# A transformer-style layer kernel on one core: x loaded first, conditioning row chunks shared out differently, late columns placed amid lower steps

## The reference, cut to what matters

```python
c_act = jax.nn.silu(c)
mod = (c_act @ w_ada[l] + b_ada[l])[:, None, :]
sh_m, sc_m, g_m, sh_f, sc_f, g_f = jnp.split(mod, 6, axis=-1)
u = layer_norm(x) * (1 + sc_m) + sh_m
z = u @ w_in[l]
```

## Time and profile before

| | us |
|---|---|
| median of 3 runs | 1427.4 (1426.52 to 1428.69) |
| the profiled execution, its own time | 1426.88 |
| its span in the trace | 1425.1 |
| TensorE busy in the span | 1393.0 (98%) |
| VectorE / ScalarE / GpSimd busy | 969.4 / 647.3 / 421.8 |

### The profile page before, as it was taken

One profiled execution on the slowest core, in us unless ns is written; L12 is line 12 of the kernel. 1 busy time (PEld: TensorE's weight loads), 2 busy tenths in 40 slices (PEclk: granted clock), 3 DMA queues, 4 the chain that ended last, 5 costly groups with the idle time before them and its releaser, 6 DMA issues.

```text
span 1425.1 us, 17299 instructions
## 1 busy us (share of the span) xinstructions
PE 1393.0 (98%) x6522; PEld 1148.6 (81%) x6522; DVE 969.4 (68%) x1340; ACT 647.3 (45%) x914; POOL 421.8 (30%) x453
## 2 busy tenths in 40 slices
PE   7799999999999999999999999999999999999996
PEld 3688888888888888888888888888888888888885
DVE  5789677776479946464768797556565646437787
ACT  5522677777542124101616774443345535343251
POOL 1006465555566000000024327333444200001315
PEclk9899999999999999999999999999999999999998
DMA  9775465654565232762622555444445878456361
GB/s 347 266 266 159 148 185 156 188 168 149 161 234 172 89 104 79 245 192 86 200 114 89 183 181 193 142 145 146 156 163 207 297 277 299 162 211 236 118 222 60
DMA packets 159083, 256.42 MB, mean 180 GB/s; under 512 B 11352, under 2 KB 81422, under 8 KB 159000
## 3 DMA queue, kind: packets, MB, share of 16 engines
q1 hardware_dynamic: 144152, 204.97, 43.1%
q0 software_dynamic: 14848, 50.34, 10.5%
HBM read 182.36 MB, written 68.71 MB: 176 GB/s over the span
## 4 chain that ended last, share of the span: by engine, by line
PE 91%; DVE 5%; ACT 2%; issue 1%; DMA 1%; SPq 0%; DVEq 0%; ACTq 0%
PE ps L2065 24%; PE ps L2067 24%; PE ps L2066 24%; PE ps L2214 11%; PE ps L2254 2%; PE ps L2264 2%; PE ps L2279 2%; PE ps L2085 1%; DVE part_lo L1922 1%; PE ps L2129 1%; PE ps L2404 1%; DVE q L1983 0%; DMA k_raw<-tw_scratch 0%; DMA ada<-in_w_ada_dram 0%; DVE w_lo L1387 0%
## 5 line engine op out<-in xcount | busy, mean ns | idle before, releaser
L2065 PE MATMUL ps<-act_hi,w_hi 128*128 128x512 f32 (+1 forms) x480 | 187.2, 390 | 9.4 <-DVE act_lo L1482 9.4
L1922 DVE TENSOR_TENSOR part_lo<-k_raw,part_hi 128x1024 fp32r<-128x1024 f32 x112 | 146.1, 1332 | 58.6 <-ACT part_hi L935 55.4
L2067 PE MATMUL ps<-act_hi,w_lo 128*128 128x512 f32 (+1 forms) x480 | 184.6, 385 | 0.0
L2066 PE MATMUL ps<-act_lo,w_hi 128*128 128x512 f32 (+1 forms) x480 | 184.6, 385 | 0.0
L2065 PE MATMUL ps<-part_hi 128*128 128x512 f32 x448 | 174.3, 389 | 0.0
L2066 PE MATMUL ps<-part_lo,part_hi 128*128 128x512 f32 x448 | 174.3, 389 | 0.0
L2067 PE MATMUL ps<-part_hi,part_lo 128*128 128x512 f32 x448 | 174.3, 389 | 0.0
L935 ACT ACTIVATE part_hi<-k_raw 128x1024 fp32r<-128x1024 f32 x112 | 116.4, 1059 | 113.6 <-DMA k_raw<-tw_scratch 48.8
L2065 PEld LDWEIGHTS ps<-act_hi,w_hi 128*128 128x128 f32 x480 | 91.1, 190 | 28.4 <-issue 5.9
L1387 DVE TENSOR_TENSOR w_lo<-w_raw,w_hi 128x1024 fp32r<-128x1024 f32 x51 | 65.9, 1291 | 65.6 <-ACT w_hi L935 65.6
L2066 PEld LDWEIGHTS ps<-act_lo,w_hi 128*128 128x128 f32 x480 | 91.2, 190 | 18.4 <-issue 1.0
(11 more groups left out here) (260 smaller groups left out, 3202.4 us busy)
## 6 DMA issues: line engine op xcount, KB each, us to landing
k_raw<-h_scratch SPq DMA_DIRECT2D x112, 256.0 KB, 4.2
w_raw<-in_w_in_dram SPq DMA_DIRECT2D x42, 512.0 KB, 4.1
ada<-in_w_ada_dram SPq DMA_DIRECT2D x8, 2048.0 KB, 9.6
tw_rows<-in_w_ff_dram POOLq DMA_DIRECT2D x64, 256.0 KB, 4.1
tw_scratch<-tw_sum POOLq DMA_DIRECT2D x32, 512.0 KB, 3.7
h_scratch<-h_sum POOLq DMA_DIRECT2D x64, 256.0 KB, 3.0
k_raw<-tw_scratch SPq DMA_DIRECT2D x64, 256.0 KB, 5.4
pair_raw<-in_w_ff_dram SPq DMA_DIRECT2D x13, 1024.0 KB, 6.3
```

Source lines behind the costliest of these rows:

```text
L1922: nc.vector.tensor_tensor(part_lo[s][:, :, :], k_raw[rs][:, :, :], f(part_hi[s][:, :, :]), ALU.subtract)\
L2065: nc.tensor.matmul(out, sh, mh, start=first, stop=False)
L2066: nc.tensor.matmul(out, sh, ml, start=False, stop=False)
L2067: return nc.tensor.matmul(out, sl, mh, start=False, stop=last)
```

## The change

- SP loads all of x ahead of chunk 0. Weight block 1 goes ahead of chunk 1, and block 2, which waits for VectorE's first `cut_lo`, ahead of chunk 3.
- TensorE turns tiles 0 to 4 first, then chunk 0's first half, tiles 5 and 6, its second half, tile 7, the small rows, six of chunk 2's eight rows, and the columns of 0 and 2. Behind them stand 24 transposes of the identity into a bank that nothing reads, in three groups of 8; the second group waits for `mod_done` 1, the third for the first `modulate_x`.
- The last two rows of chunk 2 are summed on VectorE; `row_columns(2)` adds both parts, 8 small matmuls in place of 4.
- Chunk 3 is split: rows 0 to 3 on TensorE behind the lower steps of blocks 0 and 1, rows 4 to 7 on VectorE. `row_columns(3)` has 8 small matmuls in place of 4. The columns of 1 and 3 stand after two of block 2's four lower steps.
- ScalarE and VectorE go tile by tile instead of by pairs; tiles 6 and 7 are both copied by VectorE.

The diff, cut to its core:

```diff
-N_DIRECT = 2
+N_DIRECT = 1
+SPLIT = {0: 4, 1: 4, 2: 6, 3: 4}
...
-ADA_BANKS = {0: 0, 2: 1}
+ADA_BANKS = {0: 0, 2: 1, 3: 6}
...
                 elif i == 4:
-                    sp.wait_ge(partial_done, 1)
+                    sp.wait_ge(partial_done, 2)
                 elif i == 5:
                     sp.wait_ge(head_ps_done, 4)
+                    sp.wait_ge(partial_done, 1)
                 elif i == 6:
-                    sp.wait_ge(partial_done, 2)
+                    sp.wait_ge(head_ps_done, 5)
+                    sp.wait_ge(partial_done, 3)
...
-                ks = slice(4 * half, 4 * half + 4)
+                ks = (slice(0, SPLIT[i]), slice(SPLIT[i], 8))[half]
...
-            load_ada_half(0, 0)
-            load_x(range(2))
-            load_ada_half(0, 1)
-            load_x(range(2, 4))
+            load_x(range(ST))
+            load_ada(0)
...
-            load_ada_half(2, 0)
-            load_x(range(4, 6))
-            load_ada_half(2, 1)
-            load_x(range(6, ST))
+            load_ada(2)
             load_block(0)
+            load_block(1)
             load_ada(1)
-            load_block(1)
+            load_block(2)
             load_ada(3)
-            load_block(2)
...
-            for i in range(0, ST, 2):
+            for i in range(ST):
                 take_root(i, i)
-                take_root(i + 1, i + 1)
-                norm(i, i, mid[:, i, :])
-                if i + 1 < ST - 1:
-                    norm(i + 1, i + 1, mid[:, i + 1, :])
-                if i == 2:
-                    save_ada_row(0)
-                if i == ST - 2:
-                    save_ada_row(2)
-                    cut_hi(0)
-                    save_tile(i)
-                else:
-                    save_tile(i)
-                    save_tile(i + 1)
+                if i >= 1:
+                    norm(i - 1, i - 1, mid[:, i - 1, :])
+                if i >= 2:
+                    save_tile(i - 2)
+            save_ada_row(0)
+            save_ada_row(2)
+            cut_hi(0)
...
             cut_hi(2)
+            save_ada_row(3)
             act.wait_ge(mod_done, 2)
...
-            for i in range(0, ST, 2):
-                for t in (i, i + 1):
-                    dve.wait_ge(x_in[t], 16)
-                    stats(mid[:, t, :], t)
-                for t in (i, i + 1):
-                    scale_bias(t, t)
-                if i == 4:
-                    dve.wait_ge(head_ps_done, 3)
-                    nc.vector.tensor_copy(cols[:, 0:ROWS_A], ps[:, 7, PIECE:PIECE + ROWS_A])
-                    nc.vector.tensor_copy(cols[:, ROWS_A:ROWS_A + ROWS_C], ps[:, 7, PIECE + P:PIECE + P + ROWS_C])\
-                        .then_inc(cols_done, 1)
+            for t in range(ST):
+                dve.wait_ge(x_in[t], 16)
+                stats(mid[:, t, :], t)
+                if t >= 1:
+                    scale_bias(t - 1, t - 1)
+            scale_bias(ST - 1, ST - 1)
...
-                dve.wait_ge(ada_in[i % 3], 16 * (i // 3 + 1))
+                if i == 1:
+                    dve.wait_ge(ada_in[1], 16)
+                elif i in (2, 3):
+                    dve.wait_ge(ada_end_in[i % 3], 16 * (i // 3 + 1))
+                else:
+                    dve.wait_ge(ada_in[i % 3], 16 * (i // 3 + 1))
...
             def end_chunk(i):
-                if i in (1, 3):
-                    dve.wait_ge(ada_end_in[i % 3], 16 * (i // 3 + 1))
-                add_rows(i, range(4, 8))
+                if i == 1:
+                    dve.wait_ge(ada_end_in[1], 16)
+                add_rows(i, range({2: 7, 3: 5}.get(i, 4), 8))
...
+            for t in (ST - 2, ST - 1):
+                dve.wait_ge(z_done, t + 1)
+                dve.wait_ge(x_copied, ST - 2)
+                nc.vector.tensor_copy(x_t[:, :, t * P:(t + 1) * P], tile_banks(t)).then_inc(x_copied, 1)
+            dve.wait_ge(head_ps_done, 3)
+            nc.vector.tensor_copy(cols[:, 0:ROWS_A], ps[:, 7, PIECE:PIECE + ROWS_A])
+            nc.vector.tensor_copy(cols[:, ROWS_A:ROWS_A + ROWS_C], ps[:, 7, PIECE + P:PIECE + P + ROWS_C])\
+                .then_inc(cols_done, 1)
+            ada_chunk(2)
             mixer_columns(0)
-            dve.wait_ge(z_done, ST)
-            nc.vector.tensor_copy(x_t[:, :, (ST - 1) * P:ST * P], tile_banks(ST - 1)).then_inc(x_copied, 1)
             cut_lo(0)
...
-                pe.wait_ge((ada_in, ada_end_in)[half][i % 3], 16)
-                for k in range(4 * half, 4 * half + 4):
+                pe.wait_ge((ada_in, ada_end_in)[half][i % 3], 32 if i == 3 else 16)
+                for k in range(4 if half else 0, 8 if half else SPLIT[i]):
                     ins = nc.tensor.matmul(ps[0:1, ADA_BANKS[i], :], c_act[:, k:k + 1], ada[i % 3][:, k, :],
-                                           start=k == 0, stop=k == 7)
+                                           start=k == 0, stop=k == (7, None, 5, 3)[i])
                 return ins
...
             def row_columns(i):
 
-                if i in (0, 2):
-                    pe.wait_ge(head_sb_done, 3 + i // 2)
-                else:
+                if i != 1:
+                    pe.wait_ge(head_sb_done, {0: 3, 2: 4, 3: 5}[i])
+                if i > 0:
+                    pe.wait_ge(partial_done, {2: 1, 1: 2, 3: 3}[i])
+                if i in (1, 3):
                     pe.wait_ge(cols_done, 1)
-                    pe.wait_ge(partial_done, 1 + i // 2)
                 for m in range(4):
                     out, ms = ps[:, 6 + i % 2, 4 * i + m:4 * i + m + 1], slice(m * P, (m + 1) * P)
-                    if i in (0, 2):
-                        ins = nc.tensor.matmul(out, ada_row[i][:, ms], ones_row[0:1, 0:1], start=True, stop=True)
-                    else:
-                        ins = nc.tensor.matmul(out, partial_of(i)[:, ms], ones_row[:, 0:1], start=True, stop=True)
+                    if i != 1:
+                        ins = nc.tensor.matmul(out, ada_row[i][:, ms], ones_row[0:1, 0:1], start=True, stop=i == 0)
+                    if i > 0:
+                        ins = nc.tensor.matmul(out, partial_of(i)[:, ms], ones_row[:, 0:1], start=i == 1, stop=True)
                 ins.then_inc(reduced, 1)
...
+            for i in range(5):
+                transpose_x(i)
             pe.wait_ge(head_sb_done, 2)
             row_chunk(0, 0)
-            transpose_x(0)
-            transpose_x(1)
+            transpose_x(5)
+            transpose_x(6)
             row_chunk(0, 1).then_inc(head_ps_done, 1)
-            transpose_x(2)
-            transpose_x(3)
+            transpose_x(7)
             pe.wait_ge(small_in, SMALL_ROWS)
...
-            row_chunk(2, 0)
-            transpose_x(4)
+            row_chunk(2, 0).then_inc(head_ps_done, 1)
             row_columns(0)
-            transpose_x(5)
-            row_chunk(2, 1).then_inc(head_ps_done, 1)
-            transpose_x(6)
             row_columns(2)
-            transpose_x(7)
+
+            def keep_active():
+                for m in range(8):
+                    nc.tensor.transpose(ps[:, 0, m % 4 * P:(m % 4 + 1) * P], ident[:, :], ident[:, :])
+
+            keep_active()
+            pe.wait_ge(mod_done, 1)
+            keep_active()
+            pe.wait_ge(u_step, 1)
+            keep_active()
 
             def rows_part(n, k):
                 pe.wait_ge(u_lo_done, k + 1)
@@ -2167,11 +2176,15 @@
             for n in range(2):
                 for k in range(2, 4):
                     rows_part(n, k)
+            pe.wait_ge(mod_done, 1)
+            row_chunk(3, 0).then_inc(head_ps_done, 1)
             pe.wait_ge(w_lo_done, 3)
-            for k in range(4):
+            for k in range(2):
                 rows_part(2, k)
             row_columns(1)
             row_columns(3)
+            for k in range(2, 4):
```

More of the change, by code:

```diff
@@ L962, in save_ada_row @@
             def save_ada_row(i):
-                act.wait_ge(head_ps_done, {0: 1, 2: 4}[i])
+                act.wait_ge(head_ps_done, {0: 1, 2: 4, 3: 5}[i])
                 copy(ada_row[i], ps[0:1, ADA_BANKS[i], :]).then_inc(head_sb_done, 1)
@@ L1434, in start_chunk @@
                     dve.wait_ge(reduced, i - 3)
-                link(nc.vector.tensor_scalar(partial_of(i)[:, :], ada[i % 3][:, 0, :], c_act[:, 0:1], None, ALU.mult))
-                add_rows(i, range(1, 4))
+                k0 = SPLIT[i] if i in (2, 3) else 0
+                link(nc.vector.tensor_scalar(partial_of(i)[:, :], ada[i % 3][:, k0, :], c_act[:, k0:k0 + 1], None,
+                                             ALU.mult))
+                add_rows(i, range(k0 + 1, 4))
             def end_chunk(i):
-                if i in (1, 3):
-                    dve.wait_ge(ada_end_in[i % 3], 16 * (i // 3 + 1))
-                add_rows(i, range(4, 8))
+                if i == 1:
+                    dve.wait_ge(ada_end_in[1], 16)
+                add_rows(i, range({2: 7, 3: 5}.get(i, 4), 8))
             def add_rows(i, ks):
@@ L2174, in _ @@
             row_columns(3)
```

(2 more changed lines are left out.)

## The result

The changed kernel takes 1431.97 us (median of 8 runs, 1430.70 to 1433.91) against 1427.34 (8 runs, 1426.52 to 1428.69) for the kernel before: ratio 1.0032, 95% interval 1.0022 to 1.0042. It is slower by 4.6 us (3.1 to 6.0). The forecast was 1431.6, slower. The traced execution of the changed kernel took 1432.93 us with a span of 1431.1, 6.0 more than the span before; so its trace shows the loss a little large.

A forecast was written before the change was run, and what follows sets the result against it. TensorE, busy almost throughout, was taken as the bound, so delays in the early stages reach the end almost whole. Head 3.8 plus late columns 0.4 gave 4.2 us, hence 1431.6 us; own range 1430.0 to 1433.0, with rivals 1428.8 to 1435.2.

The forecast's parts named there:

- The head: Stages up to the first `modulate_x`: this would start at 39.55 us, 3.8 later than 35.77.
- S: Moment when TensorE starts tile 4 of x, forecast at 19.55 us; behind it TensorE is the bound.
- whole list behind S: TensorE's work from tile 4 through the columns of 0 and 2, claimed to take 19.5 us.
- hand-over to `modulate_x`: Time from the end of TensorE's list to the first `modulate_x`, claimed as 0.5 us.
- T: Start of ScalarE's first `modulate_x`, 35.77 us before, forecast 39.55; everything behind is measured by its distance from it.
- The lower steps: Steps behind the first `modulate_x`: zero saved by the fillers, since TensorE waits for `act_lo` of k = 3 anyway.
- The late columns: Columns of 1 and 3 ahead of the steps from k = 4: net 0.4 us later, bounds -1.0 to +1.7.
- (a): Rival: half clock in the new row block at S costs 1.6 to 2.9 us, giving 1433.2 to 1434.5; chance 0.22.
- (b): Rival: x normalised as it lands, S 15.5 to 18.2, result 1427.5 to 1430.2; chance 0.20 with the filler rule.
- (c): Rival: a gain, needing T below 32.5 or a saving behind 67 us; chance 0.06.
- (d): Rival: clock falls in the 1.4 us hole, or chunk 3's half waits for its load; up to 1.7, inside (a)'s figures.
- The wait for k = 3: Sign: TensorE waits for `act_lo` of k = 3 some 13 us after T, longer than 0.56.

The follow-up runs named there:

- grouped: Changed kernel with the 8 small matmuls of `row_columns(2)` and (3) reordered, four from the copied row first, then four from VectorE's sum: 1431.21 us, ratio 1.0022.
- after_chunk1: Changed kernel with VectorE's first half of chunk 1 summed earlier, in its idle time ahead of `mixer_columns(0)`: 1431.59 us, ratio 1.0029 to the kernel before.
- no_fillers: Changed kernel without the 24 transposes of the identity: 1432.38 us, ratio 1.0035 to the kernel before.
- late_only: Kernel before with only chunk 3 split (rows 0 to 3 on TensorE) and the late columns amid block 2's lower steps: 1429.38 us, ratio 1.0011.
- head_only: Changed kernel with chunk 3 whole on VectorE and the late columns back behind all four lower steps of block 2: 1433.10 us, ratio 1.0032.
- cols_apart: The grouped kernel with chunk 1's columns between block 2's first and second step, chunk 3's behind the second: 1432.13 us, ratio 1.0028 to the kernel before.
- row_cut: Changed kernel with chunk 0's second half done with one row matmul in place of four: 1429.96 us, ratio 1.0018 to the kernel before.
- row_first: Changed kernel with chunk 0's first half loaded ahead of x again and its row work first in TensorE's list: 1436.23 us, ratio 1.0056.
- early_chunk1: Kernel before with chunk 1's first half summed in VectorE's idle time, tile 7 ahead of chunk 2's columns, late columns before block 2's last lower step: 1422.59 us, 0.9966.

## Why the prediction was right

**The head: right in its mechanism and, by luck of signs, in its size.** 3.8 us were forecast, 4.1 measured: S came 1.1 sooner and the list behind it took 1.2 longer than forecast. Term by term:

| | forecast | measured |
|---|---|---|
| tile 0 of x is there | 5.5 | 4.92 |
| ScalarE per tile | 2.4 | 2.12 |
| TensorE starts tile 4 (S) | 19.55 | 18.48 |
| tile 4 | 1.02 | 1.75 |
| columns of 0 and 2 | 2.80 | 3.40 |
| whole list behind S | 19.5 | 20.65 |
| hand-over to `modulate_x` | 0.5 | 0.75 |
| T | 39.55 | 39.88 |

The pace of ScalarE was overrated: back to back the square root takes it 0.09 and not 0.2, the norm 1.13 and the copy 0.92, less than half a pair. The four tiles ahead of S were "about 4 us of work" for TensorE and kept it busy for 6.5, which its waits for ScalarE hid. The list was underrated by the paired small matmuls (grouped, 0.5 us) and by tile 4 (0.7). The hand-over grew by VectorE's two operations on `mod`, 0.46 apart instead of 0.20 (0.20 again in after_chunk1, where VectorE had been idle for 3.5 us ahead of them and not for 6.3; no run tells why).

**The lower steps: right.** Zero saved by the fillers, at T + 13.1 the same wait. no_fillers shows it, and after_chunk1 shows what sets that time. What the fillers won in the trace went into the wait for block 1's `w_lo`, ahead of the one that I had named.

**The late columns: right in sign on the old head (late_only); the size stays open.** +0.4 was forecast. Against the trace of before it is 5.4 - 4.1 = 1.3; late_only gives 1.6 (0.3 to 2.9); against head_only's trace it is 0.3, and in the ratios of these two nothing. What parts these figures, as far as the traces tell, is how long half clock lasted behind the columns in each execution. Two terms of the sum were too small in the changed kernel's own trace: the small matmuls, again (3.3 for 2.7), and the first matmul of block 2, 0.43 for 0.23. These put the columns' end at T + 27.2 instead of T + 26.4. And the idle time of 1.4 at full clock turned out as half clock without idle time. That cost next to nothing: the steps from k = 4 start within 0.2 us of their `act_lo`. In after_chunk1's trace it came out as forecast, a hole of 1.27 us at full clock.

**The rivals.** (a), half clock in the row block: it came, earlier than I had put it. The clock was down in tiles 3 and 4 and up again by the first row half (3.52), so that it cost 0.7 and not 1.6 to 2.9; in head_only, grouped and cols_apart tile 4 took 1.1 and it cost nothing. One premise of (a) is weaker than it reads: through the 6.40 us of the first half chunk the profile grants 1.00, and half clock there is inferred from the length alone. The same holds for the first tile here, 1.95 us at a grant of 1.00. (b), x normalised as it lands: ScalarE's list kept 2.1 us a tile, as I argued. (c) did not occur; there is a gain to be had in this stretch, but by another edit. (d) did not come as a wait: chunk 3's loads were there.

**What I had said would show it.** T at about 39.5: 39.88. ScalarE at 2.3 to 2.4 us a tile: 2.1. No gap from 19.5 to 39: none. The wait for k = 3 longer than 0.56: 0.79. A hole of 1.4 with no half clock: neither in this trace, both in after_chunk1's.

## What to carry to other kernels

Before moving loads of the critical input forward, write down what the bounding engine would do until that input is ready: here TensorE gave up the gapless work that it had from 7.16 on, most of it on the rows, did 6.5 us of tiles until 18.48, and had all the row work behind them. Price work that comes onto a full engine against the idle time it removes, and look first for an idle engine that could deliver earlier: summing half a chunk in VectorE's idle time, and putting the columns where they then fall, gained 4.8 us at no added work. A filler is worth nothing where the engine, once faster, waits for something else (no_fillers); no run here shows one that paid. And where half clock comes and goes between executions of one kernel, a single trace does not size a term of 1 us: take one from each side whose clock agrees, or several.

## What the runs showed of the hardware

**Half clock without a gap in TensorE's rows.** Granted clock by stretch in the changed kernel, around the late columns (stretch, us, PE busy with count, clock, DMA share, GB/s):

```profile
57.00:61.00 4.00, 4.00 (x11) 1.00 0.81 279
64.00:67.00 3.00, 3.00 (x23) 1.00 1.08 355
68.00:70.00 2.00, 2.00 (x7) 0.50 1.05 387
72.00:74.00 2.00, 2.00 (x11) 1.00 1.06 388
```

TensorE's rows are gapless throughout, yet half clock is granted right behind 3.3 us of small matmuls, and likewise behind the first such stretch, at 40.3. The late stretch has the same in the traces of late_only, no_fillers, grouped, row_cut, cols_apart and row_first. But such a stretch does not always bring it: in after_chunk1, with TensorE's list unchanged and both stretches 3.3 us long, the grant is 1.00 throughout. In early_chunk1, with 1.7 us of small matmuls, it held through 2.6 us of idle time as well. By the Trainium skill, "TensorE: Matmul & The Clock Gate", Part 1, activity releases the throttle; the trace of before agrees where TensorE had been idle ahead of a fall; these falls, behind rows without a gap, that part of the page does not explain. No run isolates their cause.

**A small matmul's price depends on its neighbour.** With one column moving, 0.245 us each in a row of equals from one-row weights, 0.21 from full weights alone, 0.31 in pairs of one-row and full weights that add into one column (grouped).

**The first load.** 512 KB issued at 1.21 were with VectorE at 4.92; with 1 MB ahead on the queue the same tile came at 8.91. In the kernel before, with 1 MB ahead as well, it came at 8.43. A megabyte at the start cost 3.5 and 4.0 us in these traces, and 2.8 by the rate of the stream (378 GB/s).
